# Token-wise products taken as 512 rows by 512 columns in a two-block transformer kernel on one core

## The reference, cut to what matters

```
# first block
h = h + rms_norm(merged @ w_out[l], post_mix_gain[l])
u = rms_norm(h, pre_ffn_gain[l])
...
# second block
proj = h @ w_in[l]
dq, dk, dv, dz, db, da, cq, ckv, kix, wix = jnp.split(proj, offs, axis=-1)
...
x = x + jnp.concatenate([o_dn, o_dsa], axis=-1) @ w_out[l]
hx = rmsnorm(x, g_xattn[l])
...
kvx = (mn @ w_xkv[l]).reshape(b, m_len, 2, X_HEADS, X_DH)
...
x = x + ox @ w_xo[l]
```

## Time and profile before

| | |
|---|---|
| time, median of 3 runs | 989.95 us (989.78 to 990.08) |
| time of the profiled execution | 992.74 us |
| its span | 990.7 us |
| PE busy | 967.3 us (98% of the span), 6772 matmuls |
| PE weight loads | 884.1 us |
| DVE busy | 692.5 us (70%) |
| ACT busy | 536.6 us (54%) |
| POOL busy | 131.0 us (13%) |
| mean memory traffic | 156 GB/s |

### The profile page before, as it was taken

The page is one execution under the profiler, slowest core; times in us unless marked ns, Lnnn a source line. Parts: engine busy times, 40 slices in busy tenths (PEclk is TensorE's granted clock), DMA queues, the critical chain, the costliest instruction groups (busy, mean ns, idle before and its releaser), DMA issues.

```text
span 990.7 us, 16714 instructions
## 1 busy us (share of the span) xinstructions
PE 967.3 (98%) x6772; PEld 884.1 (89%) x6772; DVE 692.5 (70%) x1280; ACT 536.6 (54%) x1035; POOL 131.0 (13%) x145
## 2 busy tenths in 40 slices
PE   9999999999999999999999999999899999999997
PEld 8999898999999988888989999888799998888886
DVE  6887776776478676767576779966665477667675
ACT  7776767764456644444445885544444364444443
POOL 2211111211042000000010139611100000000001
PEclk9999999999999999999999999989999999999999
DMA  9533333434358555555657642201352365656551
GB/s 324 180 128 129 128 128 128 129 128 145 123 173 263 173 197 186 191 192 185 199 182 236 213 129 85 86 1 43 129 170 86 112 208 176 200 179 199 182 169 42
DMA packets 126107, 154.91 MB, mean 156 GB/s; under 512 B 2728, under 2 KB 117680, under 8 KB 125648
## 3 DMA queue, kind: packets, MB, share of 16 engines
q1 hardware_dynamic: 123616, 142.91, 43.7%
q0 software_dynamic: 1952, 10.55, 3.0%
q10 hardware_dynamic: 464, 0.40, 0.2%
HBM read 150.69 MB, written 3.16 MB: 155 GB/s over the span
## 4 chain that ended last, share of the span: by engine, by line
PE 80%; DVE 9%; ACT 7%; POOL 2%; issue 2%; DMA 1%; POOLq 0%; DVEq 0%; ACTq 0%
PE ps L785 13%; PE ps L761 7%; PE ps L786 7%; PE ps L763 7%; PE ps L762 7%; PE ps L1066 5%; PE ps L1039 4%; PE ps L1040 4%; PE ps L1041 4%; PE ps L805 3%; PE ps L807 3%; PE ps L806 3%; PE ps L747 3%; DVE wlo L1306 3%; ACT whi L1942 2%; ACT F L1942 2%
## 5 line engine op out<-in xcount | busy, mean ns | idle before, releaser
L1306 DVE TENSOR_TENSOR wlo<-raw,whi 128x1024 fp32r<-128x1024 f32 x268 | 326.6, 1235 | 176.8 <-ACT whi L1942 176.2
L1942 ACT ACTIVATE whi<-raw 128x1024 fp32r<-128x1024 f32 x268 | 274.6, 1051 | 143.1 <-PE ps L786 53.5
L785 PE MATMUL ps<-R1b,whi 128*128 128x512 f32 x576 | 201.8, 393 | 0.0
L761 PE MATMUL ps<-R1b,whi 128*128 128x256 f32 (+1 forms) x592 | 172.6, 292 | 0.8 <-DVE wlo L1306 0.8
L763 PE MATMUL ps<-R1b,wlo 128*128 128x256 f32 (+1 forms) x592 | 167.7, 283 | 0.0
L762 PE MATMUL ps<-R1b,whi 128*128 128x256 f32 (+1 forms) x592 | 167.5, 283 | 0.0
L786 PE MATMUL ps<-R1b,wlo 128*128 128x256 f32 x576 | 161.4, 280 | 0.0
L785 PEld LDWEIGHTS ps<-R1b,whi 128*128 128x128 f32 x576 | 108.1, 188 | 24.7 <-issue 0.5
L761 PEld LDWEIGHTS ps<-R1b,whi 128*128 128x128 f32 x592 | 111.6, 188 | 9.7 <-issue 7.9
L763 PEld LDWEIGHTS ps<-R1b,wlo 128*128 128x128 f32 x592 | 111.8, 189 | 0.0
L762 PEld LDWEIGHTS ps<-R1b,whi 128*128 128x128 f32 x592 | 111.5, 188 | 0.2
(11 more groups left out here) (297 smaller groups left out, 2021.1 us busy)
## 6 DMA issues: line engine op xcount, KB each, us to landing
raw<-in_w_in SPq DMA_DIRECT2D x35, 1024.0 KB, 5.1
raw<-in_w_ffn_in SPq DMA_DIRECT2D x22, 1024.0 KB, 5.1
raw<-in_w_ffn_out SPq DMA_DIRECT2D x11, 1024.0 KB, 5.4
raw<-in_w_gate SPq DMA_DIRECT2D x11, 1024.0 KB, 5.3
raw<-in_w_up SPq DMA_DIRECT2D x11, 1024.0 KB, 5.4
raw<-in_w_down SPq DMA_DIRECT2D x11, 1024.0 KB, 5.6
raw<-in_w_out SPq DMA_DIRECT2D x8, 1024.0 KB, 5.2
raw<-in_w_xkv SPq DMA_DIRECT2D x8, 1024.0 KB, 5.6
```

What stands on the lines that cost most here:

```text
L761: e.matmul(o, hi[:, kt, c], R[0][:, kt, 0:n], start=kt == 0, stop=False)
L785: e.matmul(B[:, :].rearrange("p (a n) -> p a n", a=2), hi[:, kt, c], R[2][:, :, kt, 0:256], start=kt == 0, stop=False)
L1306: e.tensor_tensor(half_of(wlo[i % HL], i, k), half_of(raw[i % RAW], i, k), f32(half_of(whi[i % HL], i, k)), SUB).then_inc(lo_split(i, (i, k)))
L1942: return e.activation(o, i, f, **kw)
```

## The change

All tok units become 512 rows (four k-tiles) by 512 columns, and a PSUM bank then holds one token tile's 512 columns. Two units, one above the other, finish a half of the columns. A unit's bytes, its half's splits and the number of units stay. There are 480 matmuls of 512 columns (464 for `tail`) where there were 960 of 256 (and 208). The copies, the tanh, the squares and the additions behind them are on 512 columns of one tile, and come only after the second unit. In `w_out`, `w_out_2` and `w_xo_2` the last unit does all of its rows for token tile 0 and then for tile 1, so its two halves both have to be split before; the additions, turns and squares are placed between and behind. The chunks behind `w_out` now alternate with splits. In `MIX` (position, side, step; side -1 is ahead of the product at the position, 1 behind it) three steps of the index move: `pre2` from ahead of product 10 to behind it, `pre3` from behind 10 to ahead of 12, `index` 0 from ahead of 11 to behind it. So `index` 0 now stands ahead of `pre3`, and ahead of it on PE are one product half, `pre2` and another product half, where there were `pre2`, a product half and `pre3`.

```diff
-    (4, -1, "pre0", 0), (4, 1, "pre0b", 0), (6, 1, "vr", 0), (7, -1, "pre0c", 0), (8, 1, "pre1", 0), (10, -1, "pre2", 0), (10, 1, "pre3", 0), (11, -1, "index", 0),
+    (4, -1, "pre0", 0), (4, 1, "pre0b", 0), (6, 1, "vr", 0), (7, -1, "pre0c", 0), (8, 1, "pre1", 0), (10, 1, "pre2", 0), (12, -1, "pre3", 0), (11, 1, "index", 0),
...
-    def outs(name, w, s, first):
-
-        yield from crossed("tok", [(("out", name, u), name, 256 * u) for u in range(4)], first, (
-            [], [], [], [], [("add", w, 0)], [("add", w, 1), ("turnx", s, 0)],
-            [("add", w, 2), ("turnx", s, 1), ("squares", w, 0)], [("add", w, 3), ("turnx", s, 2), ("squares", w, 1)]))
...
+    def halved(token, i, *then):
+
+        for j in range(2):
+            take(i, j)
+            step(*token, j, i)
+            for s in then[j] if then else ():
+                step(*s)
+            yield 1
+
+    def tiled(token, i, *then):
+
+        for t in range(2):
+            ahead(taken=-2 * t)
+            if t == 0:
+                halves.extend(((i, 0), (i, 1)))
+            step(*token, None, i, (t,))
+            for s in then[t]:
+                step(*s)
+            yield 1
+
+    def outs(name, first=((), ()), left=((), ()), right=((), ())):
+
+        order.extend((name, "tok", (k, 512 * c), 512) for k in range(2) for c in range(2))
+        i = len(order) - 4
+        yield from halved(("out", name, 0), i, *first)
+        yield from halved(("out", name, 1), i + 1, (("rows", "nm"),) if name == "w_out" else (), ())
+        yield from halved(("out", name, 0), i + 2, *left)
+        yield from tiled(("out", name, 1), i + 3, *right)
...
-    step("psq", 3)
     step("post", "p1")
...
-    for u in range(4):
-        step("chunk", u)
-    fill(2)
+    step("chunk", 0)
+    step("chunk", 1)
+    fill(1)
+    step("chunk", 2)
+    fill(1)
+    step("chunk", 3)
...
-    mix = [unit(("tail", 0), "w_in_2", "tok", 2048), unit(("tail", 1), "w_in_2", "tok", 2304, 208)]
+    mix = [wide(("tail", 0), "w_in_2", 2048, 464)]
...
-    zg = [unit(("zg", u), "w_in_2", "tok", 1536 + 256 * u) for u in range(2)]
+    zg = [wide(("zg", 0), "w_in_2", 1536)]
...
+            def tok(B, i, t, ks, R, ready):
 
                 hi, lo = unit(i)
+                at, n, c = order[i][2][0], order[i][3], slice(128 * t, 128 * t + 128)
+                for k in ks:
+                    kt = 4 * at + k
+                    p.wait_ge(*ready(kt, t))
+                    e.matmul(B[:, 0:n], R[0][:, kt, c], hi[:, k, :], start=kt == 0, stop=False)
+                    e.matmul(B[:, 0:n], R[0][:, kt, c], lo[:, k, :], start=False, stop=False)
+                    m = e.matmul(B[:, 0:n], R[1][:, kt, c], hi[:, k, :], start=False, stop=kt == 7)
+                return m
...
-                    a.wait_ge(gemm, ("mem", (1, 3)))
+                    a.wait_ge(gemm, ("mem", (1, 1)))
...
-                pool.wait_ge(mem_act, (1, 3))
+                pool.wait_ge(mem_act, (1, 1, 1))
```

More of the change, by code:

```diff
@@ L205, in alike @@
 def alike(order, i):
-    a, b = [("tok" if form == "featk" else form, n) for _, form, _, n in (order[i], order[i - HL])]
+    a, b = [("feat", n) if form == "feat" else ("rows", {"featk": 4, "tok": 2, "rows": 4}[form] * n)
+            for _, form, _, n in (order[i], order[i - HL])]
     return a == b
@@ L263, in paired @@
+    def paired(name, w, s):
+        i = tokens(name, 0)
+        take(i, 0)
+        halves.append((i, 1))
         for t in range(2):
-            for u in range(2):
-                step("out", name, u, 0, i0 + u, (t,))
+            for j in range(2):
+                step("out", name, 0, j, i, (t,))
                 yield 1
[L267 to L273, removed]
+        yield from halved(("out", name, 0), i + 1, (), [("add", w, 0, 0), ("add", w, 0, 1)])
+        i = tokens(name, 512)
+        yield from halved(("out", name, 1), i, [("turnx", s, 0)], [("turnx", s, 1), ("squares", w, 0)])
+        yield from tiled(("out", name, 1), i + 1, [("add", w, 1, 0)], [("add", w, 1, 1)])
@@ new lines, in tok, with two @@
+                return m
+            def two(kind, u, part, i, pool, R, ready, freed):
+                at = order[i][2][0]
+                if (at, part) == (0, 0):
+                    for t in range(2):
+                        claim(pool, (kind, u, t), freed(t))
+                p.wait_ge(lo_split, (i, part))
+                for t in range(2):
+                    m = tok(ps(kind, u, t), i, t, (2 * part, 2 * part + 1), R, ready)
+                m.then_inc(gemm(("half", i, part), ("unit", i), (kind, u)))
@@ L1003, in out_ @@
             def out_(name, u, part, i, tiles=(0, 1)):
[L1004 to L1009, removed]
+                R, ready = OUT[name]
+                ends = order[i][2][0] == 1
+                p.wait_ge(lo_split, (i, 1 if part is None else part))
+                for t in tiles:
+                    if not ends and part == 0:
+                        claim(f"bank{2 * u + t}", (name, u, t), (post_dve, ("p1", "v")) if name == "w_out" else (add_dve, (name, u, t)))
+                    m = tok(ps(name, u, t), i, t, range(4) if part is None else (2 * part, 2 * part + 1), R, ready)
+                    keys = [(name, u, t)] if ends else []
+                    if t == 1:
+                        keys += [("half", i, j) for j in ((0, 1) if part is None else (part,))] + [("unit", i)]
+                    if keys:
+                        m.then_inc(gemm(*keys))
             def mem(vals, u, part, i):
                 if vals:
-                    two("mem", (1, u), part, i, "four", R3b, 256, normed("nm"), (mem_act, (1, u)))
+                    two("mem", (1, u), part, i, "four", R3b, normed("nm"), lambda t: (mem_act, (1, u, t)))
                 else:
@@ L2379, in post @@
             def post(w):
-                n = 4 if w == "p1" else 2
+                n = 2
                 for t in range(2):
```

128 lines of the change are left out of this document (57 added, 71 removed).

## The result

The changed kernel took 986.37 us (median of 6 runs, 985.71 to 987.28), the kernel before 990.02 in the same measurement. The medians differ by 3.7 us. The ratio is 0.9952, with a 95% interval of 0.9941 to 0.9963, which makes it 4.7 us (3.7 to 5.8). The forecast was 985.1, with a range of 979.0 to 988.8. The profiled execution took 987.28, its span is 985.5.

The account below looks back on a forecast made before the run. PE's matmul stream and PE's waits were taken to bound the kernel, with DVE the bound from 597 us. The terms summed to -4.8 us: 992.74 to 987.9 profiled, 985.1 for the median; range 979.0 to 988.8.

Parts of the forecast that it names:

- A: The forecast itself: 985.1 us, half of the loss at index 0 swallowed, clock cost included; chance 0.42.
- C: Rival: the wait at index 0 is kept in full, with the clock, nothing taken back; 986.7 us, chance 0.17.
- term 4: Values' second half, tail and mixer to index 0: PE waits 4.2 us, half the loss swallowed, clock 1.6; +3.1 us.
- D: Rival: a 512-column matmul runs at 0.240 us, so pairs save nothing; 989.3 or 991.0 us, chance 0.08.
- D2: Rival: a pair saves only a fifth of the 11.7 ns; 988.5 us, chance 0.04.
- Term 1: w_out: 96 pairs save 1.1 us and the wait for R2l goes; -2.3 us.
- Term 2: Behind w_out: squares stand ahead of the split and chunks start earlier, gaining only PE's short waits; -0.5 us.
- term 3: The first 48 pairs of the memory's values, PE alone: -0.6 us.
- B: Rival: the wait at index 0 doesn't come or the DVE-bound stretch takes it all up; 981.3 us, chance 0.24.
- Terms 5 and 6: At 646.59 the wait for SA goes with the tanh, -0.7 us; zg's 48 pairs, half counted, -0.3 us.
- Terms 7 and 8: w_out_2: 96 pairs, -1.1 us; w_xo_2: 96 pairs and two waits, for the last head's copy and X, -2.4 us.

Follow-up runs that it names:

- experiment three: The changed kernel in its whole order, with each tok matmul of 512 columns issued as two of 256: 991.64 us, ratio 0.9996 to the kernel before.
- experiment seven: The changed kernel, with PE waiting ahead of w_out's first matmul for k-tiles 2 and 3 of R2l: ratio 0.9999 to the kernel before.
- experiment eight: The changed kernel with the four chunks behind w_out in a row and two product halves behind them: ratio 0.9989 to the kernel before.
- experiment four: The changed kernel with unread matmuls on PE ahead of index 0's wait: 44 took 997.54 us (ratio 1.0063), 14 took 985.67 us (0.9938).
- experiment one: The changed kernel with the three index steps (pre2, pre3, index 0) back at their old places: 981.33 us, ratio 0.9896 to the kernel before.
- experiment two: The kernel before, with only the three index steps moved to the changed kernel's places: ratio 1.0038, 3.8 us slower.
- experiment five: The changed kernel with only pre2 back at its old place: 981.68 us, ratio 0.9903 to the kernel before.

## Why the prediction was right

The sign and the size held, and the median lies within the stated range. The likeliest case was A at 985.1; the median, 986.37, lies closer to C at 986.7. The two differ in term 4 alone, and there C's mechanism is what happened. The terms, one by one:

**Pitch.** 0.0117 us for a pair was forecast, 0.0129 was measured. Experiment three shows 4.4 us of time from it. D and D2 fell: D wanted 0.240 for a matmul of 512 columns, and D2 a saving of a fifth of the forecast. The Trainium skill ("TensorE: Matmul & The Clock Gate", "Wait — 56ns, not 53.3ns?") gives about 2.5 ns as what a matmul takes beyond its columns. The trace does not agree with it: a pair saved 12.9 ns here.

**Term 1** (-2.3 forecast, -2.4 measured). Shown in both halves by experiments three and seven.

**Term 2** (-0.5 forecast, -1.1 measured). The mechanism was right, the size was taken from PE's marked waits alone. Experiment three has 12.81 us here (306.36 to 319.17), so the 1.1 is all order. The marks in brackets are too short, since they begin only behind the modelled end of the instruction before. By starts, the first eight transposes of `X` took 1.33 us before (312.67 to 314.00) and 0.79 after (310.62 to 311.41), and the next four 0.91 (316.95 to 317.86) and 0.35 (314.36 to 314.71): 0.54 and 0.56, together the 1.1, where the marks gave 0.21 and 0.31. Experiment eight shows that the alternation, which I had priced at nothing, is worth 3.5 there.

**Terms 3 and 4** (+2.5 forecast, +4.6 measured). The wait at `index` 0 and the half clock came as forecast in kind. The wait was 6.05 where I had 4.2, for two reasons. Counted from the stage's start, PE reached `index` 0 2.5 us earlier than before (568.20 - 514.65 = 53.55, against 574.47 - 3.55 + 3.03 - 517.85 = 56.10), where I had 1.2 beside term 3; and the exponentials ended only 0.25 earlier (54.84 against 55.09), where I took 0.7 out of bounds of 0 to 1.2: the write went out 1.24 earlier (38.15 against 39.39), but took 10.84 instead of 9.86. A write of more than 10 us was one of my own signs of being wrong; it came, and cost about 1 us. A wider wait by an earlier PE costs nothing in the net, so the second reason counts, 0.45. The step that failed is "I take half of the loss as swallowed": of the loss by `index` 0 I had 1.5 taken back by the waits at 595 and 630. The wait at 595 (1.05) did go, but the one ahead of the chunks grew from 1.88 to 2.70, so no more than 0.2 of the two was saved. Term 4 is then 4.6 + 0.6 = +5.2, where A had +3.1 and C +4.7: for this stage C's mechanism held, the wait kept in full and the clock with it. The clock's 1.6 was right (1.55 in experiment four). And B's other half fell too: without the wait the stage is no shorter than before (experiment one).

**Terms 5 and 6** (-1.0 forecast, -2.8 in the two profiled executions). The wait for SA of 0.70 is gone as forecast, with the tanh. The rest, 1.8, came where no term was, and the runs give no ground for booking it as the change's. These windows lie behind the place of that wait, in the kernel before and in the changed one:

```profile
650.00:654.00 4.00, 4.00 (x21) 4.00 (x20) 1.57 (x4) 0.00 (x0) 0.00 (x0) 0.50 0.00 0
...
650.00:654.00 4.00, 4.00 (x27) 4.00 (x26) 2.07 (x3) 0.00 (x0) 0.00 (x0) 0.68 0.00 0
```

From 646 to 658 the granted clock was 0.74, 0.50 and 0.90 before, and 0.89, 0.68 and 1.00 after. Two groups of 16 products there took 3.76 and 3.10 us before (from 648.81 and 652.37) and 3.32 and 2.33 after (from 648.66 and 651.78). But experiment two has the units of before and the same wait, and experiment one those of the changed kernel, and in both the clock was 1.00 through the whole stretch (experiment two first):

```profile
652.40 0.38 PE L1066 MATMUL ps<-st,F 128*128 128x1 f32 x2 [0.71 <-ACT SA L1942]
636.20:701.40 65.20, 61.29 (x487) 55.62 (x487) 46.91 (x123) 33.18 (x89) 11.92 (x16) 1.00 0.10 33
...
627.40:691.40 64.00, 60.78 (x450) 53.64 (x450) 47.48 (x121) 33.17 (x89) 12.52 (x18) 1.00 0.10 34
```

The stretch takes 65.16 (636.22 to 701.38) and 64.05 (627.39 to 691.44). So at full clock in both the change is worth 1.1 here, as forecast (1.0). Against this the half clock cost 3.0 in the profiled execution of before (68.18) and 1.35 in that of the changed kernel (65.40), which is the other 1.7. The wait for SA alone doesn't bring it, since in experiment two the clock stayed up behind it. Executions of the kernel before differ in their mean clock by as much, so I take it as a difference of these two executions; that the change has no part in it is not shown.

**Terms 7 and 8** (-1.1 and -2.4 forecast, -0.8 and -3.0 measured). In `w_out_2` one wait grew from 1.24 to 1.33. Experiment three has 56.19 there (700.22 to 756.41), so the 0.8 is pitch. In `w_xo_2` both waits of the earlier trace rows are gone. In experiment three this stretch takes 221.49 (756.41 to 977.90) against 223.40, so 1.9 is order and 1.1 is pitch. Both waits are gone in experiment three too, so the order took them and not the faster stream. There one low part stands ahead of the copy on DVE, and the copy waits for PE alone:

```profile
778.17 0.69 DVE L1924 COPY F<-ps 128x512 f32<-128x512 f32 x1 [0.21 <-PE ps L784]
```

That the copy's place made the wait of 0.91 rests on this and on the earlier trace rows; no run moves the copy by itself.

So term 4 was 2.1 us too low, because nothing was swallowed. Against it stood 0.6 each in terms 2 and 8 that I had not priced, and in the profiled pair the 1.7 of clock besides. Without these 1.7 the ledger's 5.2 would be 3.5, near the 3.7 between the medians. That the total came so close to the forecast is in part luck. The one forecast that experiments turned into a better kernel is the wait at `index` 0: the changed kernel with the three index steps left where they were takes 0.9896 of the time before, about twice the gain.

## What to carry to other kernels

Price each part of a change by itself, and look for the one that takes something back: here a reordering of three small steps cost more than half of what the wider stream, the earlier chunks and the shorter waits brought, and it could be left out. When a step moves on one engine, read what now stands between it and its source on every other engine; ACT's order alone gave the wait of PE within 2 us. A wait of PE can cost more than its length: look at the granted clock behind it before pricing it, and then for a later wait that would take the loss up. Compare a stretch of two kernels only between executions with the same granted clock in it; otherwise a difference of the executions is booked as one of the change. And read what a wait cost from start to start, not from its mark.

## What the runs showed of the hardware

Behind a wait of PE the granted clock of the next 4 us was at or partly at the lower of its two levels in some cases: 0.57 after 2.28 (experiment seven), 0.59 after 1.83 (experiment eight), 0.61 after 1.88, 0.57 after 6.05 and after 2.70 (the changed kernel), 0.50 after 4.29 (experiment two). In others it was 1.00: after 1.44 at 697 (the changed kernel), after 1.64 at 635 and 1.96 at 627 (experiment one), after 1.79 at 571 (experiment five) and after 2.71 at 637 (experiment seven). It also fell at 646 to 654 in the changed kernel (0.89, 0.68), where PE has no marked wait. So the length of the wait alone does not decide it; what does stays open.

What a fall costs depends on what follows. It cost 1.5 to 1.6 us in experiments four and seven. In experiment five it cost nothing. The clock fell behind the chunks' wait of 1.98 there (first line), where it was 1.00 in experiment one, but experiment one then has a wait for DVE (second line) that experiment five has not:

```profile
628.00:632.00 4.00, 4.00 (x24) 3.71 (x24) 3.93 (x6) 1.68 (x4) 4.00 (x6) 0.65 0.36 90
...
635.29 0.49 PE L1109 MATMUL ps<-F,SA 128*128 128x128 f32 x2 [1.64 <-DVE st L1345]
```

The stretch of the chunks takes 64.03 (627.71 to 691.74) in experiment five and 64.05 in experiment one.

A write of 2 MB on POOL's queue took 9.7 to 9.9 us beside the old stream's loads (before, experiments two and three) and 10.2 to 11.6 beside those of the wide stream (the changed kernel and eight other runs), though the bytes are the same. Three of the latter run the same code up to the write and took 10.84 (the changed kernel), 10.2 (experiment four with 44 matmuls) and 11.07 (with 14), so up to 0.9 of such a difference is no work of an edit. What makes the rest wasn't tried.
